# A 64x64 triangular inverse put together from two 64x64 factors in three visits instead of from 32x32 quarters in four

## The chip, the core and the metric

The kernel runs on one core of a Trainium2 chip. The metric is the device time of one execution in microseconds. The profile is one execution taken by the hardware profiler. Engines: PE is TensorE (matmuls), PEld its weight loads, DVE is VectorE, ACT is ScalarE, POOL is GpSimd. SP (SyncE) and ACT also issue DMAs, from their queues SPq and ACTq.

## What is computed

One block of a hybrid sequence model on 256 tokens of width 2048, in float32. The input is normalised and multiplied by a wide matrix; three branches follow (an RWKV-7 branch, a Mamba-2 branch, a short convolution), each is projected and gated, and the sum is projected again, added to the input and normalised. Only the RWKV-7 branch is touched by the change. Its recurrence is, for each of 16 heads of width 64:

```
def step(s, inp):
    r_t, w_t, k_t, v_t, kh_t, b_t = inp
    sa = jnp.einsum('bhvk,bhk->bhv', s, kh_t)
    s = s * w_t[:, :, None, :] - sa[..., None] * b_t[:, :, None, :] + v_t[..., None] * k_t[:, :, None, :]
    return s, jnp.einsum('bhvk,bhk->bhv', s, r_t)
```

The kernel does it in chunks of 64 tokens. Inside a chunk the term with `sa` couples each token to the earlier ones, so a strictly lower triangular 64x64 system has to be inverted for each head and chunk.

## The kernel before

**The main stream.** PE works through the big projections in "half chunks": eight matmuls on one tile of weights, four pairs of a 512-column product with the high parts (line 1353) and a 256-column product with the low parts (line 1356). A half chunk is one slot `t`; a main iteration `j` has 40 slots and handles one 128-channel tile, that is two heads (e) of the RWKV branch. There are seven such iterations in a loop and an eighth written out (`main(j, False)`, `main(CT - 1, True)`). Weights come in by DMA from SP into a ring of four buffers `raw`; ACT rounds them to `whi` (line 454, 128x1024) and DVE subtracts to get `wlo` (line 848, 128x1024), once in every two slots. All engines run their own program in the order in which it is written; semaphores tie them.

**The branch work hangs between the slots.** After some half chunks PE makes a short "visit": a handful of small float32 matmuls for the recurrence. A visit belongs to slot `t`, and the waits of the visit (`ready_behind(t)`) stand ahead of the last `wlo` matmul of that half chunk, so that a late partner holds the main stream itself. `V_P1` is 18.

**The inverse.** Each iteration has two heads (e), two blocks of 128 tokens (b) and two chunks in each (c). The four groups (b, e) are numbered q. For each chunk the 16x16 diagonal blocks are inverted on DVE in 32 partitions (`solve_step`, `solve_corner`; the last write is the copy of line 1155, semaphore `sol_tr`). The results and their transposes lie in `sol_2` and are spread over 128 partitions by DMA into `tb`: SP issues two DMAs (line 303) and ACT two (line 603), each 128 runs of 128 bytes. DVE multiplies `tb` by the block mask `par` to get `tx` (line 1078), block diagonal in 32 columns (two 16x16 blocks). From there:

- slot 18: `p1` = off-diagonal scores (`s4`) times the transposed small inverses, 32x32 (line 1584); before it the visit does `rk_mm` (1571) and `xv_mm` (1578); DVE adds the identity (1088)
- slot 19: the 32x32 inverses and their transposes (1593, 1596); ACT and DVE copy them out (673, 201)
- slot 20: `g_mm` (1605), slot 21: `h_mm` (1615), the lower left 32x32 quarter of the 64x64 inverse; ACT copies each (681, 684)
- slot 22: `uw_mm` (1623) uses the finished 64x64 inverse `t64`.

DVE in the same slots also does the causal convolution (864), the bonus products (1091, 1093), `shift` (881), `fold` (854), the gate of z (1168) and the segment products (1039).

Of the kernel before, what the change touches and what calls it, by code (L numbers as in the profile page):

```python
# [13 lines left out]
P = 128  # L14
D = 2048
T = 256
# [48 lines left out]
def build_program(nc, x, norm_w, w_in, rw_mu, rw_w0, rw_w2, rw_a0, rw_a2, rw_kk, rw_ka, rw_rk, rw_ln_w, rw_ln_b,  # L65
# [3 lines left out]
    with ctx:  # L69
# [52 lines left out]
        tx = lot(28).rearrange("p (q w n) -> p q w n", q=4, w=2)  # L122
        p1 = lot(29)[:, 0:P].rearrange("p (q n) -> p q n", q=4)
# [35 lines left out]
        par = sb("par", [P, 2, BLK])  # L159
        id32 = sb("id32", [P, 32])  # L160
# [10 lines left out]
        adt = sb("adt", [P, 4, CL])  # L171
        ad = sb("ad", [P, 4, BLK])
        t64 = sb("t64", [P, 4, 64])
        zeros = sb("zeros", [P, 256 + NC * (CL + 1)])
        t1, g1 = (zeros[:, n * P:(n + 1) * P].rearrange("p (q n) -> p q n", q=4) for n in range(2))
# [21 lines left out]
        def quad(n):  # L197
            return slice(32 * n, 32 * n + 32)

        def block_at(copy, i, *function):  # L200
            return copy(t64[quad(i), :, 32 * (i % 2):32 * (i % 2) + 32].rearrange("p (e b) n -> p e b n", e=2),
                        ps[quad(i), 4:6, 0:64].rearrange("p e (b n) -> p e b n", b=2), *function)

# [21 lines left out]
        names = """zeros_z f_sum z_ok pad_z const_z const_b const_m const_o prm_t prm_ok prm_d x_sq x_rt x_rs x_n x_tr h_hi h_lo ranks_sh lr_ok  # L225
# [3 lines left out]
            ad_ok n_in sol_p sol_r sol_tr t_in tx_ok p1_mm p1_ok d_mm t1_ok t64_ok  # L229
            xv_mm xv_ok g_mm g_ok h_mm h_ok uw_mm uw_ok yz_mm yz_ok z_in nm_mm  # L230
# [8 lines left out]
        def _(sp):  # L239
# [46 lines left out]
            def main(j, last):  # L286
# [15 lines left out]
                for q in range(2):  # L302
                    sp.dma_start(tb[:, q, :, :], sol_2[8 * q:8 * q + 8, :, :, :]).then_inc(s["t_in"], 16)
# [51 lines left out]
        def _(pool):  # L355
# [52 lines left out]

            pool.wait_ge(s["sc_mm"], NG)
            gp.memset(t64[:], 0.0).then_inc(s["pad_z"], 1)  # L410
# [15 lines left out]
        def _(act):  # L426
# [161 lines left out]
            def main(j, last):  # L588
# [8 lines left out]
                for t in range(2 * (LAST + GATES) if last else SLOTS):  # L597
                    if t % 2 == 0 and t // 2 < nchunks and t != 24:
                        split(t // 2 + AHEAD)
                    if t == 16:  # L600
                        act.wait_ge(s["sol_tr"], j + 1)
                        for q in range(2, 4):
                            act.dma_start(tb[:, q, :, :], sol_2[8 * q:8 * q + 8, :, :, :]).then_inc(s["t_in"], 16)
# [211 lines left out]
        def _(dve):  # L815
# [25 lines left out]
            v.tensor_reduce(id32[:], ident[:].rearrange("p (a n) -> p n a", a=4), AX.X, ALU.add)  # L841
            v.tensor_reduce(par[:].rearrange("p h u -> p (h u)"), m16b.rearrange("p (a n) -> p n a", a=4), AX.X, ALU.add
# [146 lines left out]
            def main(j, last):  # L989
# [45 lines left out]

                def seg_times(e, b):
# [6 lines left out]
                for t in range(2 * (LAST + GATES) if last else SLOTS):  # L1043
# [725 lines left out]
```

## Time and profile before

| | |
|---|---|
| median of 3 runs | 1118.74 us (1118.48 to 1118.74) |
| span of the profiled execution | 1119.5 us |
| PE busy / DVE / ACT | 99% / 72% / 55% of the span |
| chain that ended last | PE 98% of the span |
| granted TensorE clock, mean | 0.997 |

The profile gives for its execution the span from the first to the last instruction; no separate device time is shown for it, and the median of the runs lies 0.8 us below the span.

### The profile page before, as it was taken

To read this page: it belongs to the slowest core of one execution; us is meant where nothing else is said; L and a number is where in the kernel's file an instruction comes from. 1 tells how busy PE (TensorE), PEld (TensorE's weight loads), DVE (VectorE), ACT (ScalarE), POOL (GpSimd) and SP (SyncE) were. 2 spreads that over 40 slices of the span, in tenths; PEclk is the share of its full clock that TensorE was granted. 3 is DMA by queue.
4 is the path that set the end of the run, shared out by engine and by line. 5 is a ranking of instruction groups with operands and counts; after the bars stand their busy time and mean duration, and the time that the engine had idled before them with its cause. 6 is when DMAs were issued, how large, how long until landed. Compare 5 with 4: busy or idle time off the path is not lost.

```text
span 1119.5 us, 23001 instructions
## 1 busy us (share of the span) xinstructions
PE 1106.4 (99%) x8054; PEld 923.2 (82%) x8054; DVE 802.8 (72%) x1243; ACT 611.5 (55%) x931; POOL 44.4 (4%) x72
## 2 busy tenths in 40 slices
PE   8999999999999999999999999999999999999997
PEld 6888888888888888888888788888888888888885
DVE  4788889888897988879888857545555555556564
ACT  5656576565756657566565645444344444435443
POOL 3000000000000000000000030000000000000000
PEclk9999999999999999999999999999999999999999
DMA  7666656566465564756556464766666576657663
GB/s 199 188 170 170 176 136 174 158 169 165 131 172 161 157 176 124 192 146 173 145 156 182 141 203 151 225 191 196 196 189 192 164 225 192 199 182 279 200 194 107
DMA packets 254412, 197.25 MB, mean 176 GB/s; under 512 B 23095, under 2 KB 206624, under 8 KB 253856
## 3 DMA queue, kind: packets, MB, share of 16 engines
q1 hardware_dynamic: 251604, 195.81, 60.2%
q10 hardware_dynamic: 2764, 0.85, 0.3%
q8 instruction: 27, 0.44, 0.2%
q14 instruction: 17, 0.14, 0.0%
HBM read 193.71 MB, written 2.11 MB: 175 GB/s over the span
## 4 chain that ended last, share of the span: by engine, by line
PE 98%; DMA 0%; ACT 0%; SPq 0%; DVE 0%; issue 0%
PE ps L1353 31%; PE ps L1356 15%; PE ps L1452 12%; PE ps L1454 12%; PE ps L1453 12%; PE ps L1739 3%; PE ps L1738 3%; PE ps L1740 3%; PE ps L1486 1%; PE ps L1663 1%; PE ps L1336 1%; PE ps L1522 0%; PE ps L1383 0%; DMA o<-in_x 0%; PE ps L1623 0%; PE ps L1687 0%
## 5 line engine op out<-in xcount | busy, mean ns | idle before, releaser
L848 DVE TENSOR_TENSOR wlo<-raw,whi 128x1024 fp32r<-128x1024 f32 (+1 forms) x356 | 437.4, 1241 | 215.0 <-ACT whi L454 212.9
L1353 PE MATMUL ps<-hx,whi 128*128 128x512 f32 (+1 forms) x1440 | 522.9, 405 | 0.0
L454 ACT ACTIVATE whi<-raw 128x1024 fp32r<-128x1024 f32 (+1 forms) x356 | 370.3, 1051 | 252.7 <-PE ps L1454 178.7
L1356 PE MATMUL ps<-hx,wlo 128*128 128x256 f32 (+1 forms) x1440 | 404.1, 281 | 0.0
L1353 PEld LDWEIGHTS ps<-hx,whi 128*128 128x128 f32 (+1 forms) x1440 | 269.1, 187 | 70.2 <-issue 5.4
L1356 PEld LDWEIGHTS ps<-hx,wlo 128*128 128x128 f32 (+1 forms) x1440 | 270.8, 188 | 0.4
L1452 PE MATMUL ps<-whi,hx 128*128 128x512 f32 x384 | 150.3, 391 | 0.0
L1454 PE MATMUL ps<-whi,hx 128*128 128x512 f32 x384 | 149.5, 389 | 0.0
L1453 PE MATMUL ps<-wlo,hx 128*128 128x512 f32 x384 | 149.4, 389 | 0.0
L1452 PEld LDWEIGHTS ps<-whi,hx 128*128 128x128 f32 x384 | 72.1, 188 | 15.0 <-issue 0.2
L1454 PEld LDWEIGHTS ps<-whi,hx 128*128 128x128 f32 x384 | 72.1, 188 | 15.0
L1453 PEld LDWEIGHTS ps<-wlo,hx 128*128 128x128 f32 x384 | 72.1, 188 | 14.8
L1454 PE MATMUL ps<-whi,olo 128*128 128x512 f32 x192 | 74.7, 389 | 0.0
L1452 PE MATMUL ps<-whi,ohi 128*128 128x512 f32 x192 | 74.7, 389 | 0.0
L1453 PE MATMUL ps<-wlo,ohi 128*128 128x512 f32 x192 | 74.7, 389 | 0.0
L1738 PE MATMUL ps<-whi,hx 128*128 128x512 f32 x128 | 50.0, 390 | 0.0
L1740 PE MATMUL ps<-whi,hx 128*128 128x512 f32 x128 | 49.8, 389 | 0.0
L1739 PE MATMUL ps<-wlo,hx 128*128 128x512 f32 x128 | 49.8, 389 | 0.0
L1453 PEld LDWEIGHTS ps<-wlo,ohi 128*128 128x128 f32 x192 | 36.0, 188 | 7.5
L1452 PEld LDWEIGHTS ps<-whi,ohi 128*128 128x128 f32 x192 | 36.0, 188 | 7.5
L1454 PEld LDWEIGHTS ps<-whi,olo 128*128 128x128 f32 x192 | 36.0, 188 | 7.4
L467 ACT ACTIVATE lots<-ps 128x256 f32<-128x256 f32 x48 | 17.5, 382 | 39.5 <-issue 20.1
(281 smaller groups left out, 1040.3 us busy)
## 6 DMA issues: line engine op xcount, KB each, us to landing
raw<-in_w_in SPq DMA_DIRECT2D x548, 256.0 KB, 3.2
raw<-in_w_branch SPq DMA_DIRECT2D x96, 256.0 KB, 3.8
raw<-in_w_out SPq DMA_DIRECT2D x64, 256.0 KB, 3.6
o<-in_x SPq DMA_DIRECT2D x3, 1024.0 KB, 6.1
acb<-acs_rows SPq DMA_DIRECT2D x7, 256.0 KB, 3.3
out_y<-lots SPq DMA_DIRECT2D x5, 256.0 KB, 2.6
o<-in_x SPq DMA_DIRECT2D x2, 512.0 KB, 5.3
lots<-in_final_norm_w SPq DMA_DIRECT2D x1, 1024.0 KB, 10.2
```

What stands on the lines that cost most here:

```text
L454: sc.activation(whi[:, slot, :, 0:width], raw[:, slot, :, 0:width], ACT.Copy).then_inc(hi_done, 1)
L467: sc.activation(dst, ps[:, bank + t, T:2 * T], ACT.Copy).then_inc(low_out, 1)
L848: tt(wlo[:, slot, :, 0:width], raw[:, slot, :, 0:width], whi[:, slot, :, 0:width].bitcast(F32), ALU.subtract).then_inc(lo_done, 1)
L1336: return mm(ps[:, X_BANK[k % 6], b * P:(b + 1) * P], xtok[:, b, k * P:(k + 1) * P], rdiag[:, b, :], start=True, stop=True)
L1353: mm(ps[0:rows, bank, :], whi[:, slot, k, wcol], hx[:, kt].rearrange("p a t -> p (a t)"), start=first, stop=False, skip_group_check=True)
L1356: return mm(ps[0:rows, bank, 0:T], wlo[:, slot, k, wcol], hhi[:, kt, :], start=False, stop=last, skip_group_check=True)
L1452: mm(dst, xh[:, kt, r], whi_o[:, slot, k, :], start=kt == 0, stop=False)
L1453: mm(dst, xh[:, kt, r], wlo_o[:, slot, k, :], start=False, stop=False)
L1454: op = mm(dst, xl[:, kt, r], whi_o[:, slot, k, :], start=False, stop=kt == 2 * nq - 1)
L1738: mm(dst, hhi[:, kt, r], whi_o[:, y % RING, k, :], start=kt == 0, stop=False)
L1739: mm(dst, hhi[:, kt, r], wlo_o[:, y % RING, k, :], start=False, stop=False)
L1740: op = mm(dst, hlo[:, kt, r], whi_o[:, y % RING, k, :], start=False, stop=kt == KT - 1)
```

## The change

The 64x64 inverse is written as a product of two factors. With T the block diagonal of the 16x16 inverses and N the strictly-off-block part of the scores, M = T N has 4x4 blocks and its fourth power vanishes, so that the inverse is (1 + M^2)(1 + M) T. Every product is now 64x64 by 64, on the four 64x64 quarters of the array.

- `tx` becomes block diagonal in 64 columns: its own buffer, written 128x512 instead of 128x256. `par` has four columns of blocks instead of two.
- Slot 18: line 1584's 16 products of 32x32 go; in their place 16 products of 64x64 (`m_mm`: M and its transpose for all eight chunk-heads).
- Slot 19: the visit goes (24 products of 32x32), and so do its four copies; ACT copies M and its transpose out (`mx`, 128x512), DVE adds the identity (`mi`, 128x256). DVE no longer makes `p1`.
- Slot 20: 16 products of 64x64 (`k_mm`: M^2 and (1 + M) T) in place of 8 of 32x32.
- Slot 21: 8 products of 64x64 (`t_mm`) in place of 8 of 32x32. Before it ACT copies `kg` (128x256) and DVE makes 1 + M^2 (`m2i`, 128x256); after it ACT copies `t64` (128x256) in one piece.
- The rows of `tb` for odd heads have to lie on the other half of the partitions for one of the two kinds, so that one of the two DMAs of SP, and one of ACT, is split in three: SP and ACT issue four DMAs each instead of two.
- The zeroing of `t64` by POOL at the start goes.

```
                 sp.wait_ge(s["sol_tr"], j + 1)
-                for q in range(2):
-                    sp.dma_start(tb[:, q, :, :], sol_2[8 * q:8 * q + 8, :, :, :]).then_inc(s["t_in"], 16)
+                sp.dma_start(tb[:, 0, :, :], sol_2[0:8, :, :, :]).then_inc(s["t_in"], 16)
+                sp.dma_start(tb[:, 1, 1, :], sol_2[8:16, :, 1, :]).then_inc(s["t_in"], 16)
+                for h in range(CPB):
+                    sp.dma_start(tb[side(1 - h), 1, 0, :], sol_2[8 + 4 * h:12 + 4 * h, :, 0, :]).then_inc(s["t_in"], 16)
...
                     if t == V_P1 + 1:
+                        act.wait_ge(s["m_mm"], j + 1)
+                        sc.activation(mx.rearrange("p e w b n -> p e (w b n)"), ps[:, 4:6, 0:T], ACT.Copy).then_inc(s["mx_ok"], 1)
                         act.wait_ge(s["xv_mm"], j + 1)
                         act.wait_ge(s["bon_ok"], j + 1)
                         sc.activation(xx4[:, :, 1:3, :].rearrange("p b e n -> p e b n"),
                                       ps[:, 6:8, 0:P].rearrange("p e (b n) -> p e b n", b=2), ACT.Copy).then_inc(s["xv_ok"], 1)
-                        act.wait_ge(s["d_mm"], j + 1)
-                        for i in (0, 2):
-                            op = sc.activation(t1[quad(i), :, :], A[quad(i), 64:64 + P].rearrange("p (q n) -> p q n", q=4), ACT.Copy)
-                        op.then_inc(s["t1_ok"], 1)
-                        act.wait_ge(s["pad_z"], 1)
-                        for i in (0, 2):
-                            op = block_at(sc.activation, i, ACT.Copy)
-                        op.then_inc(s["t64_ok"], 1)
                     if t == V_P1 + 3:
-                        act.wait_ge(s["g_mm"], j + 1)
-                        sc.activation(g1.rearrange("p (e b) n -> p e (b n)", e=2), ps[:, 6:8, 0:64], ACT.Copy).then_inc(s["g_ok"], 1)
-                        act.wait_ge(s["h_mm"], j + 1)
-                        for i in (0, 2):
-                            op = sc.activation(t64[quad(i), :, 32:64], A[quad(i), 0:P].rearrange("p (q n) -> p q n", q=4), ACT.Copy)
-                        op.then_inc(s["h_ok"], 1)
+                        act.wait_ge(s["k_mm"], j + 1)
+                        sc.activation(kg, blocks(6, 0), ACT.Copy).then_inc(s["kg_ok"], 1)
+                        act.wait_ge(s["t_mm"], j + 1)
+                        sc.activation(t64[:], blocks(4, 0), ACT.Copy).then_inc(s["t64_ok"], 1)
...
-                        dve.wait_ge(s["t_in"], j * 64 + 64)
-                        tt(tx.rearrange("p q w (h u) -> p (q w) h u", h=2),
-                           tb[:].rearrange("p q w u -> p (q w) u").unsqueeze(2).broadcast_to([P, 8, 2, BLK]),
-                           par[:].unsqueeze(1).broadcast_to([P, 8, 2, BLK]), ALU.mult).then_inc(s["tx_ok"], 1)
+                        dve.wait_ge(s["t_in"], j * 128 + 128)
+                        tt(tx[:].rearrange("p q w (h u) -> p (q w) h u", h=4),
+                           tb[:].rearrange("p q w u -> p (q w) u").unsqueeze(2).broadcast_to([P, 8, 4, BLK]),
+                           par[:].unsqueeze(1).broadcast_to([P, 8, 4, BLK]), ALU.mult).then_inc(s["tx_ok"], 1)
...
                     if t == V_P1 + 1:
 
-                        dve.wait_ge(s["p1_mm"], j + 1)
-                        tt(p1, B[:, 0:P].rearrange("p (q n) -> p q n", q=4), id32[:].unsqueeze(1).broadcast_to([P, 4, 32]),
-                           ALU.add).then_inc(s["p1_ok"], 1)
+                        dve.wait_ge(s["m_mm"], j + 1)
                         dve.wait_ge(s["rk_mm"], j + 1)
                         tt(bon[:, 0:P], C[:, T:T + P], sh[:, 2, 0:P], ALU.mult)
                         for e in range(2):
                             op = tt(bon[side(e), P:T], E[side(1 - e), T + P:2 * T], sh[side(e), 2, P:T], ALU.mult)
                         op.then_inc(s["bon_ok"], 1)
                     if t == V_P1 + 1:
-                        dve.wait_ge(s["d_mm"], j + 1)
-                        dve.wait_ge(s["pad_z"], 1)
-                        for i in (1, 3):
-                            op = block_at(v.tensor_copy, i)
-                        op.then_inc(s["t64_ok"], 1)
+
+                        dve.wait_ge(s["mx_ok"], j + 1)
+                        plus_one(mi, mx[:, :, 1, :, :]).then_inc(s["mi_ok"], 1)
+                    if t == V_P1 + 3:
+
+                        dve.wait_ge(s["k_mm"], j + 1)
+                        plus_one(m2i, blocks(4, T)).then_inc(s["m2i_ok"], 1)
...
-                    if t == V_P1 + 1:
-                        pe.wait_ge(s["p1_ok"], j + 1)
                     if t == V_P1 + 2:
-                        pe.wait_ge(s["t1_ok"], j + 1)
+                        pe.wait_ge(s["mx_ok"], j + 1)
+                        pe.wait_ge(s["mi_ok"], j + 1)
                         pe.wait_ge(s["xv_ok"], j + 1)
                     if t == V_P1 + 3:
-                        pe.wait_ge(s["g_ok"], j + 1)
-                        pe.wait_ge(s["t64_ok"], j * 2 + 2)
+                        pe.wait_ge(s["kg_ok"], j + 1)
+                        pe.wait_ge(s["m2i_ok"], j + 1)
                     if t == V_P1 + 4:
-                        pe.wait_ge(s["h_ok"], j + 1)
+                        pe.wait_ge(s["t64_ok"], j + 1)
...
-                        for q in range(4):
-                            for i in range(4):
-                                r = slice(32 * i, 32 * i + 32)
-                                op = mm(B[r, 32 * q:32 * q + 32], s4[r, q, 2 * CL + 32 * (i % 2):2 * CL + 32 * (i % 2) + 32], tx[r, q, 1, :],
-                                        start=True, stop=True)
-                        op.then_inc(s["p1_mm"], 1)
-                    if t == V_P1 + 1:
-
-                        for q in range(4):
-                            b, e = q // 2, q % 2
-                            for i in range(4):
-                                r, o = quad(i), quad(i ^ 2 * e)
-                                mm(ps[o, 4 + e, 32 * b:32 * b + 32], p1[r, q, :], tx[r, q, 0, :], start=True, stop=True)
-                            for i in (0, 2):
-                                r, x = quad(i), 64 + 32 * (2 * e + b)
-                                op = mm(A[r, x:x + 32], tx[r, q, 0, :], p1[r, q, :], start=True, stop=True)
-                        op.then_inc(s["d_mm"], 1)
-                    if t == V_P1 + 2:
-
-
                         for b in range(2):
                             for c in range(CPB):
                                 for e in range(2):
-                                    r, o = quad(2 * c), quad(2 * (c ^ e) + 1)
-                                    op = mm(ps[o, 6 + e, 32 * b:32 * b + 32],
-                                            s4[r, 2 * b + e, 2 * CL + 32:3 * CL], t1[r, 2 * e + b, :],
+                                    r, q, n = side(c), 2 * b + e, b * CL
+                                    off = s4[r, q, 2 * CL:3 * CL]
+                                    mm(ps[side(c ^ e), 4 + e, n:n + CL], tx[r, q, 1, :], off, start=True, stop=True)
+                                    op = mm(ps[side(c ^ e), 4 + e, P + n:P + n + CL], off, tx[r, q, 1, :], start=True, stop=True)
+                        op.then_inc(s["m_mm"], 1)
+                    if t == V_P1 + 2:
+
+
+                        for b in range(2):
+                            for c in range(CPB):
+                                for e in range(2):
+                                    r, n = side(c ^ e), b * CL
+                                    mm(ps[side(c), 4 + e, T + n:T + n + CL], mx[r, e, 0, b, :], mx[r, e, 1, b, :],
+                                       start=True, stop=True)
+                                    op = mm(ps[side(c), 6 + e, n:n + CL], mi[r, e, b, :], tx[r, 2 * b + e, 0, :],
                                             start=True, stop=True)
-                        op.then_inc(s["g_mm"], 1)
+                        op.then_inc(s["k_mm"], 1)
                     if t == V_P1 + 3:
 
 
-                        for q in range(4):
-                            for h in range(2):
-                                r = quad(2 * h + 1)
-                                op = mm(A[quad(2 * h), 32 * q:32 * q + 32], g1[r, q, :], t64[r, q, 32:64], start=True, stop=True)
-                        op.then_inc(s["h_mm"], 1)
+                        for b in range(2):
+                            for c in range(CPB):
+                                for e in range(2):
+                                    op = mm(ps[side(c ^ e), 4 + e, b * CL:b * CL + CL], m2i[side(c), e, b, :], kg[side(c), e, b, :],
+                                            start=True, stop=True)
+                        op.then_inc(s["t_mm"], 1)
```

The four hunks after the first are ACT, DVE (two) and the waits ahead of the last `wlo` matmul on PE; the last is the visits of PE. How the instructions then stand on the engines is shown at three places; the line numbers of the changed kernel are its own.

DVE, from the split of slot 18 to the split of slot 20. Before:

```order
L848 TENSOR_TENSOR wlo<-raw,whi 128x1024 [waits hi_done]
L1088 TENSOR_TENSOR lots<-ps,id 128x128 [waits p1_mm]
L1091 TENSOR_TENSOR lots<-ps,lots 128x128 [waits rk_mm]
L1093 TENSOR_TENSOR lots<-ps,lots 64x128 x2
L201 COPY t<-ps 32x4x32 [waits pad_z,d_mm]
L201 COPY t<-ps 32x4x32
L847 REGISTER_ALU
L848 TENSOR_TENSOR wlo<-raw,whi 128x1024 [waits hi_done]
```

and in the changed kernel (line 1027 with `adt` is `mi`):

```order
L837 TENSOR_TENSOR wlo<-raw,whi 128x1024 [waits hi_done]
L1082 TENSOR_TENSOR lots<-ps,lots 128x128 [waits rk_mm,m_mm]
L1084 TENSOR_TENSOR lots<-ps,lots 64x128 x2
L1027 TENSOR_TENSOR adt<-lots,id 128x256 [waits mx_ok]
L836 REGISTER_ALU
L837 TENSOR_TENSOR wlo<-raw,whi 128x1024 [waits hi_done]
```

The addition of `p1` and the two copies behind `d_mm` are gone; one addition behind `mx_ok` stands ahead of the split.

DVE, from `shift` of slot 20 to the segment products of slot 21. Before:

```order
L881 SCALAR_TENSOR_TENSOR lots<-pq,prm,lots 128x256
L853 REGISTER_ALU
L854 TENSOR_TENSOR lots<-ps,lots 128x256 [waits low_out]
L853 REGISTER_ALU
L854 TENSOR_TENSOR lots<-ps,lots 128x256 [waits low_out]
L1167 REGISTER_ALU
L1168 SCALAR_TENSOR_TENSOR lots<-lots 128x256 [waits halved]
L1039 ISA [waits seg_e,dat_ok]
```

and in the changed kernel (line 1027 with `zeros` is `m2i`):

```order
L870 SCALAR_TENSOR_TENSOR lots<-pq,prm,lots 128x256
L842 REGISTER_ALU
L843 TENSOR_TENSOR lots<-ps,lots 128x256 [waits low_out]
L842 REGISTER_ALU
L843 TENSOR_TENSOR lots<-ps,lots 128x256 [waits low_out]
L1160 REGISTER_ALU
L1161 SCALAR_TENSOR_TENSOR lots<-lots 128x256 [waits halved]
L1027 TENSOR_TENSOR zeros<-ps,id 128x256 [waits k_mm]
L1032 ISA [waits seg_e,dat_ok]
```

`m2i`, for which PE waits in slot 21, stands behind the split, the shift, two folds and the gate of slot 20.

ACT, from its DMAs of slot 16 on (in the last iteration). Before:

```order
L603 DMA tb<-lots 128x1x32 [waits sol_tr]
L603 DMA tb<-lots 128x1x32
L467 ACTIVATE lots<-ps 128x256 [waits tile_done]
L467 ACTIVATE lots<-ps 128x256 [waits chunk_used]
L470 ACTIVATE lots<-xp,prm 128x256 [waits tile_out]
L645 ACTIVATE lots<-lots 128x256 [waits tile_out]
L454 ACTIVATE whi<-raw 128x1024 [waits chunk_used,raw_in3]
L669 ACTIVATE lots<-ps 128x2x2x64 [waits bon_ok,xv_mm]
L673 ACTIVATE zeros<-ps 32x128 [waits d_mm]
```

and in the changed kernel:

```order
L596 DMA tb<-lots 128x1x32 [waits sol_tr]
L597 DMA tb<-lots 128x1x16
L599 DMA tb<-lots 64x1x16 x2
L461 ACTIVATE lots<-ps 128x256 [waits tile_done]
L461 ACTIVATE lots<-ps 128x256 [waits chunk_used]
L464 ACTIVATE lots<-xp,prm 128x256 [waits tile_out]
L642 ACTIVATE lots<-lots 128x256 [waits tile_out]
L448 ACTIVATE whi<-raw 128x1024 [waits chunk_used,raw_in3]
L665 ACTIVATE lots<-ps 128x512 [waits m_mm]
L668 ACTIVATE lots<-ps 128x2x2x64 [waits bon_ok,xv_mm]
L448 ACTIVATE whi<-raw 128x1024 [waits chunk_used,raw_in0]
```

Four DMA issues stand where two stood; the copy of M (line 665) is new, and the split of slot 20 now follows directly on the copy of `xv` (line 668). SP's queue changes in the same way as ACT's, and the rest of the weights' DMAs stand behind.

## Rows read from the trace of the kernel before

**Rows 1.** The page: the span, and the chain that ended last by engine.

```profile
span 1119.5 us, 23001 instructions
...
PE 98%; DMA 0%; ACT 0%; SPq 0%; DVE 0%; issue 0%
```

**Rows 2.** Waits of PE, whole run: who for whom, us in total, times, longest.

```profile
PE ps L1336 <- DVE lots L826: 3.4, 2, 1.9
PE ps L1331 <- DVE zeros L819: 1.5, 1, 1.5
```

**Rows 3.** Timeline of PE, second iteration, slots 18 to 22: start, us, instruction, count.

```profile
200.18 0.28 PE L1356 MATMUL ps<-hx,wlo 128*128 128x256 f32 x1
200.29 0.40 PE L1353 MATMUL ps<-hx,whi 128*128 128x512 f32 x1
200.52 0.28 PE L1356 MATMUL ps<-hx,wlo 128*128 128x256 f32 x1
...
201.00 0.41 PE L1578 MATMUL ps<-lots,work 64*64 64x64 f32 x16
201.34 0.45 PE L1584 MATMUL ps<-lots,work 32*32 32x32 f32 x32
201.72 0.50 PE L1353 MATMUL ps<-hx,whi 128*128 128x512 f32 x1
...
203.12 0.28 PE L1356 MATMUL ps<-hx,wlo 128*128 128x256 f32 x1
...
203.88 0.50 PE L1353 MATMUL ps<-hx,whi 128*128 128x512 f32 x1
...
205.27 0.28 PE L1356 MATMUL ps<-hx,wlo 128*128 128x256 f32 x1
...
205.74 0.51 PE L1353 MATMUL ps<-hx,whi 128*128 128x512 f32 x1
...
207.14 0.28 PE L1356 MATMUL ps<-hx,wlo 128*128 128x256 f32 x1
...
207.72 0.51 PE L1353 MATMUL ps<-hx,whi 128*128 128x512 f32 x1
```

**Rows 4.** Timeline of DVE, the same stretch (idle time before in brackets).

```profile
199.17 0.43 DVE L1078 TENSOR_TENSOR lots<-tb,par 128x256 f32<-128x256 f32 x1 [0.91 <-DMA tb<-lots]
199.51 0.48 DVE L864 SCALAR_TENSOR_TENSOR lots<-xp,prm,lots 128x256 f32<-128x256 f32 x1
...
201.18 1.22 DVE L848 TENSOR_TENSOR wlo<-raw,whi 128x1024 fp32r<-128x1024 f32 x1
202.31 0.28 DVE L1088 TENSOR_TENSOR lots<-ps,id 128x128 f32<-128x128 f32 x1
202.52 0.28 DVE L1091 TENSOR_TENSOR lots<-ps,lots 128x128 f32<-128x128 f32 x1
202.81 0.59 DVE L1093 TENSOR_TENSOR lots<-ps,lots 64x128 f32<-64x128 f32 x2
...
206.23 1.23 DVE L848 TENSOR_TENSOR wlo<-raw,whi 128x1024 fp32r<-128x1024 f32 x1 [1.64 <-ACT whi L454]
...
208.88 1.40 DVE L1039 SCALAR_TENSOR_TENSOR lots<-lots,dat,scm 128x256 f32<-128x256 f32 x4
```

**Rows 5.** Timeline of ACT, the same stretch.

```profile
203.50 0.38 ACT L669 ACTIVATE lots<-ps 128x256 f32<-128x256 f32 x1 [3.76 <-DVE lots L1093]
...
205.13 1.06 ACT L454 ACTIVATE whi<-raw 128x1024 fp32r<-128x1024 f32 x1
```

**Rows 6.** Timeline of the two DMA queues: start, us for all issues, line, count.

```profile
196.02 1.27 ACTq L603 DMA_DIRECT2D tb<-lots  x2
...
196.02 1.53 SPq L303 DMA_DIRECT2D tb<-lots  x2
...
181.52 2.77 SPq L295 DMA_DIRECT2D lots<-ad  x4
```

**Rows 7.** Line 267, DMAs of 64 partitions: issue time in ns, min/median/max.

```profile
L267 SPq DMA_DIRECT2D lorat<-in_rw_w x8: 479/547/556, 13.3 to 545.7; - x8
```

More of the change, by code:

```diff
@@ L121, in build_program @@
         yz = flat(26, 2).rearrange("p (q n) -> p q n", q=4)
-        tx = lot(28).rearrange("p (q w n) -> p q w n", q=4, w=2)
-        p1 = lot(29)[:, 0:P].rearrange("p (q n) -> p q n", q=4)
+        mx = flat(28, 2).rearrange("p (e w b n) -> p e w b n", e=2, w=2, b=2)
+        kg = lot(32).rearrange("p (e b n) -> p e b n", e=2, b=2)
         yc, ysq = lot(29), lot(12)
@@ L158, in build_program @@
         m16b = lot(13)[:, 0:P]
-        par = sb("par", [P, 2, BLK])
-        id32 = sb("id32", [P, 32])
+        par = sb("par", [P, 4, BLK])
+        id64 = sb("id64", [P, CL])
+        tx = sb("tx", [P, 4, 2, CL])
         head1 = sb("head1", [P, P])
@@ L171, in build_program @@
         adt = sb("adt", [P, 4, CL])
+        mi = adt[:, :, :].rearrange("p (e b) n -> p e b n", e=2)
         ad = sb("ad", [P, 4, BLK])
-        t64 = sb("t64", [P, 4, 64])
+        t64 = sb("t64", [P, 2, 2, CL])
         zeros = sb("zeros", [P, 256 + NC * (CL + 1)])
-        t1, g1 = (zeros[:, n * P:(n + 1) * P].rearrange("p (q n) -> p q n", q=4) for n in range(2))
+        m2i = zeros[:, 0:256].rearrange("p (e b n) -> p e b n", e=2, b=2)
         steps = zeros[:, 256:].rearrange("p (c t) -> p c t", c=NC)
@@ L195, in side, with blocks @@
             return slice(64 * n, 64 * n + 64)
[L197 to L202, printed above, removed]
+        def blocks(bank, col):
+            return ps[:, bank:bank + 2, col:col + P].rearrange("p e (b n) -> p e b n", b=2)
         BANKS = (0, 2, 0, 0, 2)
@@ L224, in build_program @@
         low_out = sem("low_out")
-        names = """zeros_z f_sum z_ok pad_z const_z const_b const_m const_o prm_t prm_ok prm_d x_sq x_rt x_rs x_n x_tr h_hi h_lo ranks_sh lr_ok
+        names = """zeros_z f_sum z_ok const_z const_b const_m const_o prm_t prm_ok prm_d x_sq x_rt x_rs x_n x_tr h_hi h_lo ranks_sh lr_ok
             bc_s bc_th bc_ok sc_mm scm_ok dt_v dt_e dt_l dt_ae acs_ok
@@ L228, in build_program @@
             kh_ok ka_t k2_ok rk_ok rk_mm bon_ok bon_b bv_ok prod_ok tr_vk vt_ok kdbd_ok score_mm score_ok adt_ok
-            ad_ok n_in sol_p sol_r sol_tr t_in tx_ok p1_mm p1_ok d_mm t1_ok t64_ok
-            xv_mm xv_ok g_mm g_ok h_mm h_ok uw_mm uw_ok yz_mm yz_ok z_in nm_mm
+            ad_ok n_in sol_p sol_r sol_tr t_in tx_ok m_mm mx_ok mi_ok k_mm kg_ok m2i_ok t_mm t64_ok
+            xv_mm xv_ok uw_mm uw_ok yz_mm yz_ok z_in nm_mm
             nm_ok state_mm state_ok y_mm yc_ok ysq_ok var_mm var_rt ln_v oa_ok sc_cx sc_s sc_b sc_f oc_hi oc_ok x_s xs_ok z2_ok x_tr2 xst_ok
@@ L407, in main @@
                     kk_unit(j + 1)
-            pool.wait_ge(s["sc_mm"], NG)
-            gp.memset(t64[:], 0.0).then_inc(s["pad_z"], 1)
             kk_unit(0)
@@ L601, in main @@
                         act.wait_ge(s["sol_tr"], j + 1)
-                        for q in range(2, 4):
-                            act.dma_start(tb[:, q, :, :], sol_2[8 * q:8 * q + 8, :, :, :]).then_inc(s["t_in"], 16)
+                        act.dma_start(tb[:, 2, :, :], sol_2[16:24, :, :, :]).then_inc(s["t_in"], 16)
+                        act.dma_start(tb[:, 3, 1, :], sol_2[24:32, :, 1, :]).then_inc(s["t_in"], 16)
+                        for h in range(CPB):
+                            act.dma_start(tb[side(1 - h), 3, 0, :], sol_2[24 + 4 * h:28 + 4 * h, :, 0, :]
+                                          ).then_inc(s["t_in"], 16)
                     if t >= 2 * nchunks:
@@ L840, in _ @@
             stt(centre[:], head1[:], -1.0 / 64, ident[:], ALU.mult, ALU.add)
-            v.tensor_reduce(id32[:], ident[:].rearrange("p (a n) -> p n a", a=4), AX.X, ALU.add)
-            v.tensor_reduce(par[:].rearrange("p h u -> p (h u)"), m16b.rearrange("p (a n) -> p n a", a=4), AX.X, ALU.add
+            v.tensor_reduce(id64[:], ident[:].rearrange("p (a n) -> p n a", a=2), AX.X, ALU.add)
+            v.tensor_reduce(par[:].rearrange("p h u -> p (h u)"), m16b.rearrange("p (a n) -> p n a", a=2), AX.X, ALU.add
                             ).then_inc(s["const_o"], 1)
@@ L1034, in solve_corner, with plus_one @@
                     v.tensor_reduce(dst, prod, AX.X, ALU.add).then_inc(s["sol_r"], 1)
+                def plus_one(dst, src):
+                    return tt(dst, src, id64[:].unsqueeze(1).unsqueeze(1).broadcast_to([P, 2, 2, CL]), ALU.add)
                 def seg_times(e, b):
@@ L1622, in main @@
                                 for e in range(2):
-                                    op = mm(ps[side(h ^ e), 4 + e, b * P:b * P + P], t64[side(h), 2 * e + b, :],
+                                    op = mm(ps[side(h ^ e), 4 + e, b * P:b * P + P], t64[side(h), e, b, :],
                                             xx[side(h), (2 * b + e) * P:(2 * b + e) * P + P], start=True, stop=True)
```

## The prediction, written before the changed kernel ran

> **What bounds the kernel now.** I read the page first: the chain that ended last is PE for 98% of 1119.5 us [rows 1]. Then the waits of PE: in the whole run it waited twice, for 4.9 us in all, both times in the first microseconds (its first operands, zeroed and scaled by DVE) [rows 2]. In the main iterations PE never waits. So two questions decide the change: does PE's own work get shorter, and does any partner that PE has so far never waited for come too late? What nobody waits for today may be late by little, so next I read the timelines of PE, DVE and ACT for slots 18 to 22 of the second iteration, one beside the other. The other seven have the same shape; their gaps differ by under 0.2 us.
>
> **PE's own work.** A visit's cost is the gap between the last `wlo` matmul ahead of it and the first `whi` matmul behind it, less the 0.11 us that stand between the two without a visit (200.18 to 200.29) [rows 3].
> - Slot 19 goes whole: 203.12 to 203.88 is 0.76, less 0.11: -0.65.
> - Slot 18: the old 32 instructions (each float32 product is two) took 0.38 (201.34 to 201.72). Thirty-two of 64x64 stand there now. The nearest row is line 1578, the same shape on the same four quarters: 16 in 0.34 (201.00 to 201.34), 21 ns each, which includes the change to narrow products behind it. By that price it is 0.68 (+0.30); the lower bound is the 32-wide price, 12 ns (+0). That change of width goes, so I take +0.1.
> - Slot 20: 32 in place of 16. 205.27 to 205.74 is 0.47, less 0.11 is 0.36 with its start. Bounds: 16 more at 12 ns (+0.2) and 32 at 21 ns against 16 at 16 (+0.42). I take +0.3.
> - Slot 21: 16 in place of 16; before they used two tiles of the array and now use four, twice as wide. Bounds -0.2 and 0; I take -0.05.
>
> Sum: -0.3 us an iteration (bounds -0.7 and +0.05, all ends at once), over eight iterations -2.4 us. If nothing else moved, that would be all.
>
> **What the new steps wait for.** Now the partners, in order of time.
>
> *The DMAs.* `tx` waits for the `tb` DMAs: DVE stood idle 0.91 us for them, then started `tx` at 199.17 [rows 4]. Issuing is slow: two took ACT 1.27 us and two took SP 1.53 us, both from 196.02 on; four of 128 runs of 64 bytes took SP 2.77 us, 0.69 each; one of 64 partitions takes 0.547 us [rows 6, 7]. The new set on each queue is one like before, one of 128 short runs and two of 64 short runs. On SP: 0.77 + 0.69 + 2 x 0.55 = 2.56 against 1.53, so the last issue ends 1.03 us later. Bounds for what isn't shown, a short issue of 64 runs: half of 0.69 (the sum is 2.15, +0.6), and the 0.77 of an issue when both queues issue at once, for all four (3.06, +1.5). I take a delay d of 1.15 us, because both queues issue together for longer.
>
> At this place a rule of the Trainium skill speaks for a smaller price. The page "DMA: Bandwidth & Descriptors", section "Issuing engines are not separate DMA queues", says that the time an engine's sequencer needs to start a DMA is usually small relative to the DMA itself. By it the two more issues would cost nearly nothing, and the sum would be that of the second rival below; the trace does not agree for these tiny transfers, where an issue takes 0.64 to 0.77 us.
>
> *tx.* It starts at 199.17 + d and is 128x512. From 128x256 (0.43) and 128x1024 (1.22) [rows 4] it should take 0.43 + 0.26 = 0.69. PE needs it ahead of its last `wlo` matmul of slot 18, at 200.52 [rows 3]. It is there at 199.17 + 1.15 + 0.69 + 0.05 = 201.06: PE **waits 0.5 us** where it never waited.
>
> *bon, mi, xv.* DVE goes on with three convolution steps and the split of slot 18, without a gap after `tx`, so they shift by d + 0.26. Then `p1` is gone (202.31 to 202.52: -0.21) [rows 4]. The bonus products, which ended at 202.81 + 0.59 = 203.40, end at 203.45 + d = 204.60. `mi` follows, 0.43, at 205.03; the copy of `xv` on ACT (0.10 behind, 0.38 long [rows 5]) ends at 205.08. PE asks for both ahead of the last matmul of slot 20: 205.27 + 0.5 + 0.1 - 0.65 = 205.22. Just in time; a late one here would be swallowed by the next wait anyway. The copy of M on ACT (twice the width of a 0.38 us copy, begun about 202.5) is done before the bonus products are.
>
> *m2i.* This one is the crux. The order shows it behind five instructions on DVE, the first of which is the split of slot 20, which waits for ACT's `whi`; ACT does that `whi` behind the copy of `xv`. It used to stand behind the four copies of slot 19, and now comes earlier. ACT: copy ends 203.93 + d; DVE's split starts 1.10 after ACT's (205.13 to 206.23) [rows 4, 5]: 205.03 + d. From the start of that split to the first instruction behind the gate of z DVE takes 206.23 to 208.88, 2.65 us, with no wait inside [rows 4]: `m2i` starts at 207.68 + d, takes 0.43 like any 128x256, and PE has it at 208.16 + d. PE's last matmul of slot 21 stood at 207.14 [rows 3]. So PE passes this point **1.02 + d later than before**, whatever happened in slots 18 to 20: the gain of slot 19 and the wait of slot 18 are both inside. With d = 1.15 it is 2.17 late, at 209.31; it would arrive at 205.22 + 0.3 + (207.14 - 205.27) = 207.39, so **it waits 1.9 us**. Queued behind that waiting matmul is the whole main stream.
>
> *After it.* The visit of slot 21 saves 0.05. `t64` is one copy of 0.38 us, with a half chunk of 1.4 us ahead of its use. ACT and DVE lose less than PE, so their slack grows: nothing else turns late. SP issues the remaining weights of that strip about 1 us later; they are split on ACT in slots 22 and after, some 7 us behind their landing. The edits outside the loop (two reductions 64 wide instead of 32, one zeroing less on POOL) are hundredths of a microsecond.
>
> **The sum.** Per iteration 1.02 + 1.15 - 0.05 = 2.12 us; over eight 17.0. The profiled execution's span goes from 1119.5 to 1136.5; the median of the runs lies 0.8 below the span, 1118.7 + 17.0 = 1135.7.
>
> **The rivals.**
> 1. *As summed, both waits.* With d from 0.6 to 1.5, an iteration costs 1.6 to 2.5 us: 1131.3 to 1138.7. Chance 0.73.
> 2. *The DMAs are not later* (short issues cheap, or overlapped with the moving of data): d near 0 to 0.4. Then `tx` is in time and only `m2i` is late: 0.97 us an iteration, 7.8 in all: 1126.5, up to 1130. For it: the moved bytes grow by nothing. Against it: every issue row. Chance 0.11.
> 3. *Faster.* `m2i` is in time. PE without waits gets to that matmul at 207.14 - 0.65 + 0.1 + 0.3 = 206.89, so DVE would have to be 1.3 us faster than the 208.16 it needs even with d = 0; from there on only PE's sum counts, -2.4 us: 1116.3 (1113 to 1119 by the bounds). For it: it is what PE's own rows say, PE is 98% of the chain, and both ACT and DVE have idle gaps of 1.6 us and more here. Against it: the order of DVE's program, and those gaps are the ones I have already closed. Chance 0.06.
> 4. *Near no change*, the same with a wait of some tenths. Chance 0.03.
> 5. *More than summed*: small DMAs that land later still behind twice as many issues on both queues, or a wait in slot 20 or 24 as well; at 2.8 us an iteration 1141. Chance 0.07.
>
> The first case's own range is 1131 to 1139; with the upper part of the second and the nearest of the fifth it is 1127 to 1140, which leaves out about 2 in 10. About 0.2% (2.2 us) is what a measurement can tell here from no change. Slower by more: 0.73 + 0.11 + 0.07 = 0.91. Faster 0.06, same 0.03.
>
> **What the profile after would show.** Waits of PE on DVE that did not exist: one of about 0.5 us, eight times, released by the `tx` product (waited for in slot 18), and one of about 1.9, eight times, released by the addition of 1 to M^2 (slot 21). The last of the `tb` issues of SP ending about 1 us later, `tx` at about 0.69 us for 128x512. The gap of slot 19's visit closed to 0.11. If the `m2i` wait is missing, my reading of DVE's queue is wrong; if it is 1.0 to 1.5 and the first wait is missing, the DMAs were priced too high. If a wait in slot 20 shows and slot 21's is shorter by as much, the sum stands. Matmul groups 64 wide well over 21 ns an instruction would make only the waits shorter, not the time longer.

## The result

The changed kernel takes 1136.72 us (median of 5 runs, 1136.44 to 1137.94), the kernel before 1118.74 (5 runs beside it, 1118.48 to 1119.77). Ratio 1.0161, 95% interval 1.015 to 1.0173: 18 us slower, where 17 were forecast.

The page of the changed kernel, span and chain by engine, against [rows 1]:

```profile
span 1134.9 us, 22487 instructions
...
PE 81%; DVE 9%; issue 4%; DMA 2%; SPq 2%; ACT 1%; DVEq 1%; ACTq 0%
```

PE was 98% of the chain that ended last and is 81%; DVE, the DMAs and ACT have come into it. The waits of PE (who for whom, us in total, times, longest), against [rows 2]:

```profile
PE ps L1349 <- DVE zeros L1027: 10.4, 8, 1.4
PE ps L1349 <- DVE tx L1071: 5.4, 8, 0.8
PE ps L1329 <- DVE lots L815: 2.8, 2, 1.4
```

Two waits that did not exist, each eight times: for `m2i` (the addition of line 1027 into `zeros`) and for `tx`. The timeline of PE in the second iteration, against [rows 3]:

```profile
200.01 0.40 PE L1346 MATMUL ps<-hx,whi 128*128 128x512 f32 x1
201.10 0.35 PE L1349 MATMUL ps<-hx,wlo 128*128 128x256 f32 x1 [0.69 <-DVE tx L1071]
...
202.56 0.50 PE L1346 MATMUL ps<-hx,whi 128*128 128x512 f32 x1
...
205.37 0.28 PE L1349 MATMUL ps<-hx,wlo 128*128 128x256 f32 x1
205.58 0.36 PE L1588 MATMUL ps<-lots 64*64 64x64 f32 x8
...
206.26 0.50 PE L1346 MATMUL ps<-hx,whi 128*128 128x512 f32 x1
...
207.42 0.40 PE L1346 MATMUL ps<-hx,whi 128*128 128x512 f32 x1
209.12 0.35 PE L1349 MATMUL ps<-hx,wlo 128*128 128x256 f32 x1 [1.31 <-DVE zeros L1027]
209.41 0.46 PE L1599 MATMUL ps<-lots,zeros 64*64 64x64 f32 x16
209.80 0.50 PE L1346 MATMUL ps<-hx,whi 128*128 128x512 f32 x1
```

Without a wait the low product follows 0.24 us behind the high one (207.66); it came at 209.12, 1.46 us late. DVE in the same stretch, against [rows 4]:

```profile
195.33 0.38 DVE L1148 COPY lots<-lots 32x256 f32<-32x256 f32 x1
...
200.26 0.69 DVE L1071 TENSOR_TENSOR tx<-tb,par 128x512 f32<-128x512 f32 x1 [2.28 <-DMA tb<-lots]
...
204.59 0.43 DVE L1027 TENSOR_TENSOR adt<-lots,id 128x256 f32<-128x256 f32 x1
206.02 1.23 DVE L837 TENSOR_TENSOR wlo<-raw,whi 128x1024 fp32r<-128x1024 f32 x1 [1.00 <-ACT whi L448]
...
208.22 0.42 DVE L1161 SCALAR_TENSOR_TENSOR lots<-lots 128x256 f32<-128x256 f32 x1
208.56 0.42 DVE L1027 TENSOR_TENSOR zeros<-ps,id 128x256 f32<-128x256 f32 x1
```

This is the queue the forecast spoke of: M^2 is on PE's side finished before 206.26, and its addition starts at 208.56, behind the split, the shift, the folds and the gate. DVE has no idle time ahead of it after 206.02. And SP's DMA queue, against [rows 6]:

```profile
195.74 0.69 SPq L297 DMA_DIRECT2D tb<-lots  x1
196.47 0.79 SPq L298 DMA_DIRECT2D tb<-lots  x1
197.31 1.49 SPq L300 DMA_DIRECT2D tb<-lots  x2
```

The four issues end at 198.80, 3.47 us behind the copy of 195.33, instead of two at 197.55, 1.95 behind the copy of 195.60 (line 1155 in the trace of before).

**The period is the better ruler.** The last write of the small inverses (the copy of line 1155 in before, `sol_tr`) occurs once in an iteration; first and last start, seven periods apart. Of before and of the changed kernel:

```profile
L1155 DVE COPY lots<-lots x8: 384/385/387, 127.1 to 606.1; 32x256 f32<-32x256 f32 x8
```

```profile
L1148 DVE COPY lots<-lots x8: 384/386/391, 124.5 to 619.9; 32x256 f32<-32x256 f32 x8
```

68.43 us before (479.0 / 7) and 70.77 after (495.4 / 7): 2.34 us an iteration, 18.7 over eight. The changed kernel's first copy lies 2.6 us earlier than in the profile of before, which is why the span grew by only 15.4. An experiment below shows that this is the one execution of before, not the change.

### The profile page after: what moved, and what is told of

Read it like the earlier page. It is cut to its first block, busy times and chain, and to the rows that moved or that the text cites. A ratio compares the mean times of both kernels' runs of the same rounds, so it can differ in the third digit from the quotient of the medians.

```text
span 1134.9 us, 22487 instructions
## 1 busy us (share of the span) xinstructions
PE 1106.7 (98%) x7798; PEld 924.2 (81%) x7798; DVE 805.5 (71%) x1235; ACT 605.2 (53%) x899; POOL 44.1 (4%) x71
## 4 chain that ended last, share of the span: by engine, by line
PE 81%; DVE 9%; issue 4%; DMA 2%; SPq 2%; ACT 1%; DVEq 1%; ACTq 0%
PE ps L1346 21%; PE ps L1445 12%; PE ps L1446 12%; PE ps L1447 12%; PE ps L1349 11%; PE ps L1725 3%; PE ps L1723 3%; PE ps L1724 3%; DVE lots L1019 2%; DMA tb<-lots 2%; DVE wlo L837 1%; DVE lots L1008 1%; DVE lots L1010 1%; ACT whi L448 1%; DVE lots L853 1%
```

## The experiments

Periods here are worked out as above from the same copy's line in each trace.

### The addition of M^2 ahead of DVE's other work

```
+                    if t == V_P1 + 2:
+                        dve.wait_ge(s["k_mm"], j + 1)
+                        plus_one(m2i, blocks(4, T)).then_inc(s["m2i_ok"], 1)
                     if t % 2 == 0 and t // 2 < nchunks and t not in (V_ST, V_ST + 2):
                         split_lo(base + t // 2 + AHEAD, (t // 2 + AHEAD) % RING)
...
-                    if t == V_P1 + 3:
-
-                        dve.wait_ge(s["k_mm"], j + 1)
-                        plus_one(m2i, blocks(4, T)).then_inc(s["m2i_ok"], 1)
```

> The changed kernel with one addition moved: DVE makes 1 + M^2 (m2i) ahead of the weight split of slot 20 instead of behind split, shift, two folds and gate. Theory A (the wait of slot 21 is set by DVE's order): M^2 is there at about 206.4 in the second iteration, m2i at 206.9, and PE reaches its last matmul of slot 21 at 207.66 instead of 209.12. The wait on m2i goes, 1.46 us an iteration and some tenths of restart over all eight: 1124.5 to 1125.5 us. The wait for tx of 0.7 us stays. Theory B (the cost is the wider products on PE, or weights that arrive later since SP issues more): no change from 1136.7.

Measured 1124.38 us, just under the expected range, ratio to before 1.0048 (1.0033 to 1.0064), period 69.19. Of the two waits of PE in the iterations one is left:

```profile
PE ps L1348 <- DVE tx L1074: 5.4, 8, 0.8
```

One instruction's place in DVE's program was worth 12.3 us. The products, the copies and the DMAs are the same in both kernels, so theory B falls.

### Two DMAs on each queue again

```
-                sp.dma_start(tb[:, 1, 1, :], sol_2[8:16, :, 1, :]).then_inc(s["t_in"], 16)
-                for h in range(CPB):
-                    sp.dma_start(tb[side(1 - h), 1, 0, :], sol_2[8 + 4 * h:12 + 4 * h, :, 0, :]).then_inc(s["t_in"], 16)
+                sp.dma_start(tb[:, 1, :, :], sol_2[8:16, :, :, :]).then_inc(s["t_in"], 16)
```

and the same on ACT.

> The changed kernel with two tb DMAs on each queue, as before the change; the odd heads' untransposed 16x16 inverses then lie on the wrong half of the partitions, so that part of the RWKV branch is computed from other blocks. Theory A (issue time of the DMAs delays tx, and through DVE's order m2i): tx starts 1.37 us earlier, its wait on PE is gone, and m2i comes 1.37 earlier, still 1.0 us late for PE: 1125 to 1126.5 us. A rival that only the wait for tx itself counts (0.69 us an iteration) gives 1131; if the DMAs do not matter, 1136.7.

Measured 1126.25 us, ratio 1.0064 (1.0049 to 1.008), period 69.39. The wait for `tx` is gone, the one for `m2i` stays, shorter:

```profile
PE ps L1344 <- DVE zeros L1022: 6.5, 8, 0.9
```

The gain is 1.38 us an iteration, not the 0.69 of the wait that vanished: the DMAs delayed all of DVE's queue, `m2i` with it. That tells the forecast's account from the one that counts only the visible wait of slot 18 (1131). It is also the case of the forecast's second rival, DMAs that are not later: that rival had 7.8 us above the kernel before, and here are 7.5. The second iteration:

```profile
194.00 0.39 DVE L1143 COPY lots<-lots 32x256 f32<-32x256 f32 x1
...
206.43 0.36 PE L1344 MATMUL ps<-hx,wlo 128*128 128x256 f32 x1 [0.84 <-DVE zeros L1022]
```

The low product of slot 21 stands 12.43 us behind the copy of the small inverses, against 11.54 before (207.14 less 195.60).

### Both edits

> The last two edits together (the odd heads' blocks are again on the wrong half of the partitions). No wait of PE should be left, and what remains is PE's own work. The prediction's products (-0.3 us an iteration) give 1116.3; the products as the trace of the changed kernel shows them (slot 18 +0.18, slot 20 +0.42, slot 21 +0.02, slot 19 -0.65) give nearly nothing, 1117.5 to 1118.7. If a further wait was hidden behind the two, it shows here and the time stays above 1119.

Measured 1117.62 us, ratio 0.999 (0.9981 to 0.9999), period 68.24. No wait of PE in the iterations is left. Together the two edits take away 2.53 us an iteration, alone 1.58 and 1.38: less than their sum, since in `m2i_early` the DMAs' delay counts only through `tx`. What remains is PE's own work: 0.1 to 0.2 us an iteration less than before the change. The time fits the products as the trace has them, and not the forecast's -0.3 (1116.3).

### The old kernel with four DMAs on each queue

The edit of the change on its own: the second DMA split in three on SP and on ACT, with each half in its old place, and the count waited for doubled.

> The kernel before the change, the same data moved by four tb DMAs on each queue instead of two (one of 128 runs of 64 bytes and two of 64 such runs in place of the second). It shows the price of the issues alone. Theory A: tx starts 1.4 us later, at 200.5; PE waits 0.5 us in slot 18, then 0.3 to 0.4 in slot 19 for p1, which DVE makes behind it: 0.9 us an iteration, 1126 us (1124 to 1128). The rule that issuing is small beside the transfer gives no change, 1118.7.

Measured 1127.07 us, ratio 1.0071 (1.0056 to 1.0086), period 69.51, that is 1.1 us an iteration, the bytes unchanged. The split also cuts the second DMA's runs from 128 bytes to 64 and doubles their number, so the price could lie in the transfer as well. The timeline says where it lies (second iteration, SP's last two issues and `tx`):

```profile
196.46 1.51 SPq L305 DMA_DIRECT2D tb<-lots  x2
```

```profile
199.44 0.43 DVE L1083 TENSOR_TENSOR lots<-tb,par 128x256 f32<-128x256 f32 x1 [2.30 <-DMA tb<-lots]
```

From the end of the last issue to `tx` it is 1.47 us here, 1.62 in before (197.55 to 199.17): the transfers behind the last issue did not get longer, the issues alone made `tx` late. In its timeline of PE:

```profile
200.01 0.35 PE L1361 MATMUL ps<-hx,wlo 128*128 128x256 f32 x1 [0.41 <-DVE lots L1083]
...
202.45 0.39 PE L1358 MATMUL ps<-hx,whi 128*128 128x512 f32 x1
202.92 0.39 PE L1361 MATMUL ps<-hx,wlo 128*128 128x256 f32 x1
```

The wait for `tx` in slot 18, and 0.23 us more in slot 19 (0.47 from high to low product instead of 0.24) for `p1`, which DVE makes 3 us behind `tx`. The second is too short to leave idle time in the records, and shows in the starts alone. The rest, up to the 1.1, is in the two visits, which are longer behind a matmul that waited (1.28 us against 1.20 from the low product to the next high one in slot 18, 0.87 against 0.76 in slot 19).

### tx in two pieces: a complete kernel without the delay

```
-                        dve.wait_ge(s["t_in"], j * 128 + 128)
...
+                        dve.wait_ge(s["t_in"], j * 64 + 64)
+                        spread(1).then_inc(s["tx_ok"], 1)
...
+                    if t == V_P1:
+                        dve.wait_ge(s["t0_in"], j * 64 + 64)
+                        spread(0).then_inc(s["tx0_ok"], 1)
```

`spread(w)` is the product of `tx` for one w; the half DMAs count on `t0_in`; `m2i` is made early.

> A complete kernel with neither wait: m2i early, and tx made in two pieces. The first two DMAs of each queue already bring all transposed blocks (w = 1), all that slot 18 needs; DVE spreads these at once (128x256). The four half DMAs have a semaphore of their own, and DVE spreads the w = 0 blocks after the split of slot 18; PE asks for them in slot 20. Theory A: t_in is complete as early as before the change, nothing waits, the period of an iteration is that of both_waits_off (68.2 us): 1117.6 us (1117 to 1118.3), 1 us below the kernel before. If the moved half of tx (0.34 us more on DVE ahead of mi) or the later weights' DMAs of SP cost something, it is 1118.5 to 1121.

Measured 1118.56 us, ratio 0.9995 (0.9986 to 1.0004), period 68.46: no change from before that can be told, a little short of what was expected. Both big waits are gone. What is left is in DVE's timeline, second iteration:

```profile
197.91 0.48 DVE L853 SCALAR_TENSOR_TENSOR lots<-xp,prm,lots 128x256 f32<-128x256 f32 x1 [0.53 <-ACT lots L464]
...
200.72 0.42 DVE L1027 TENSOR_TENSOR tx<-tb,par 128x256 f32<-128x256 f32 x1
201.06 0.28 DVE L1092 TENSOR_TENSOR lots<-ps,lots 128x128 f32<-128x128 f32 x1
```

The first convolution step stands 0.5 us idle for the first tap, which ACT makes behind its four DMA issues, and the moved half of `tx` takes 0.34 us ahead of the bonus products (200.72 to 201.06). The second is the rival that the expectation named. The bonus products, and behind them the copy of `xv` and `mi`, are later by both, and PE's last low product of slot 20 comes 0.26 instead of 0.24 behind the high one here, more in other iterations and 0.73 in the first; the visit behind it takes 0.97 instead of 0.90.

### The order of the products

The same kernel with the loops of slots 18 and 20 turned, so that four products in a row use four quarters of the array.

> The last kernel with the products of slots 18 and 20 issued so that neighbours never use the same quarter of the array (M for all four quarters, then its transpose; M^2 for four, then the other product). In the changed kernel two products in a row use one quarter; their instructions start 67 ns apart for a round of four, where line 1578 of before has 58. If the neighbours cost that difference, 16 rounds save 0.15 us an iteration: 1116.4. If each quarter has its own queue and the order is nothing, 1117.6 as the last.

Measured 1117.88 us, ratio 0.9993 (0.9984 to 1.0002), period 68.37. The medians differ by 0.7 us, less than the intervals are wide. In the traces the 32 instructions of slot 18 stand so:

```profile
198.89 0.30 PE L1586 MATMUL ps<-work,tx 64*64 64x64 f32 x8
...
199.47 0.50 PE L1352 MATMUL ps<-hx,whi 128*128 128x512 f32 x1
```

0.58 us, against 0.67 in the changed kernel (201.89 to 202.56): the turned order saves 0.09 us there. That neighbours in one quarter cost something is what this says. What slot 18 gained PE lost again at its next wait, for `xv` and `mi` in slot 20:

```profile
202.04 0.39 PE L1352 MATMUL ps<-hx,whi 128*128 128x512 f32 x1
202.45 0.36 PE L1355 MATMUL ps<-hx,wlo 128*128 128x256 f32 x1
```

The low product comes 0.41 us behind the high one, and in both kernels it stands 9.2 us behind the copy of the small inverses. What the order is worth where nothing waits is seen in `late_halves`.

### The kernel before once more

> The kernel before, unchanged, profiled once more. The profile of before reached its first solved blocks (line 1155) at 127.1 us, all later kernels at 124.5 to 125.7, though their code ahead of it is nearly the same. If that is chance of one execution, it is near 124.6 here, and the span is about 1117; if the constants of the changed kernel make the start faster, it stays at 127.1 and the span at 1119.5.

Measured 1118.65 us. The profile:

```profile
span 1116.5 us, 23001 instructions
```

with the first copy at 124.6 and a period of 68.37 (603.2 less 124.6, by 7). So the first profile of before had a start slower by 2.5 us by chance; the median of the runs does not have it. Its main iterations agree within 0.06 us a period, and its low products of slots 18 to 21 stand at the same places behind the copy within 0.05 us. It also sets the forecast's step from span to time right: the time of a run is some 1.7 us above its span (1118.24 and 1116.5 here, 1136.66 and 1134.9 for the changed kernel), and not 0.8 below it, as the first profile beside the median had suggested. The forecast started from the median, so its time is untouched; its span, 1136.5, was not met by the measured 1134.9.

### The halves issued later

```
-                        for h in range(CPB):
-                            act.dma_start(tb[side(1 - h), 3, 0, :], sol_2[24 + 4 * h:28 + 4 * h, :, 0, :]
-                                          ).then_inc(s["t0_in"], 16)
...
                         first_tap(j, xp, cv)
+                        for h in range(CPB):
+                            act.dma_start(tb[side(1 - h), 3, 0, :], sol_2[24 + 4 * h:28 + 4 * h, :, 0, :]
+                                          ).then_inc(s["t0_in"], 16)
...
                         plus_one(mi, mx[:, :, 1, :, :]).then_inc(s["mi_ok"], 1)
+                        dve.wait_ge(s["t0_in"], j * 64 + 64)
+                        spread(0).then_inc(s["tx0_ok"], 1)
```

> tx_in_two_order with what its trace showed late put right: ACT issues its two half DMAs behind the first tap of the convolution instead of ahead of it (DVE stood idle 0.55 us for that tap, and PE then waited 0.1 to 0.2 us in slot 20 for the copy of xv), and DVE spreads the w = 0 blocks behind mi instead of ahead of the bonus products. Theory A: no wait of PE is left in the main iterations, the period falls from 68.3 to 68.1 or 68.2 us: 1117.0 us (1116.3 to 1117.6), 1.5 us below the kernel before. If the halves now land too late for slot 20, PE waits there for tx0 and the time is 1118 or more.

Measured 1115.88 us (9 runs, 1115.37 to 1117.16), ratio 0.9971 (0.9961 to 0.9981), period 68.11: faster than both kernels, more so than expected. In its timeline of PE, second iteration, the visit of slot 20 and its neighbours:

```profile
201.65 0.28 PE L1354 MATMUL ps<-hx,wlo 128*128 128x256 f32 x1
201.86 0.34 PE L1595 MATMUL ps<-lots 64*64 64x64 f32 x8
...
202.49 0.50 PE L1351 MATMUL ps<-hx,whi 128*128 128x512 f32 x1
```

and on ACT the copy of `xv`, and on DVE `m2i` waiting for PE, not the other way round:

```profile
200.24 0.39 ACT L668 ACTIVATE lots<-ps 128x256 f32<-128x256 f32 x1 [0.61 <-DVE lots L1091]
```

```profile
202.62 0.43 DVE L1033 TENSOR_TENSOR zeros<-ps,id 128x256 f32<-128x256 f32 x1 [1.69 <-PE ps L1600]
```

The bonus products start 6.63 us behind the copy of the small inverses, and 7.57 in `tx_in_two`: the 0.53 of the tap and the 0.34 of the half are both gone. From low product to next high one the visit of slot 20 takes 0.84 us, against 0.90 in `both_waits_off`, and that of slot 18 takes 1.29 against 1.39: with no wait left, the turned order shows in the period, 68.11 against 68.24. The two kernels differ in the DMAs and in `tx` too, and this one has two edits at once, so how much of the 3.1 us below before belongs to the order, to the later halves and to the later piece of `tx` was not measured one by one. Issuing the half DMAs from POOL's queue instead was not tried.

## Why the prediction was right

**PE passes slot 21 late by 1.02 + d.** Measured from the copy of the small inverses, the low product of slot 21 stood 11.54 us behind it before (207.14 less 195.60, where line 1155 starts in the first trace) and 13.79 after (209.12 less 195.33): 2.25 late; forecast 2.17. With the visit behind it 2.34 an iteration, forecast 2.12. `m2i_early` shows the wait is the order's, and its removal gives 1.58. The mechanism was right; that the number is as near as 0.08 is in part luck. d was 0.21 larger than forecast, and the 1.02 was 0.89: `dma_two`, where `tx` starts 3.57 us behind the copy as before and d is nothing, shows the same 0.89 (12.43 less 11.54). The 0.13 between are three small terms: DVE's split of slot 20 started 0.10 earlier than worked out (10.69 us behind the copy), DVE took 2.54 us from it to `m2i` (206.02 to 208.56) and not 2.65, and PE started 0.56 behind the start of `m2i` (209.12) and not 0.48.

**d, the delay of the DMAs: a term too small.** `tx` started 3.57 us behind that copy before and 4.93 after: 1.36, not 1.15. The step that was off is the price of an issue of 64 runs, taken as 0.55 from line 267: here the median is 0.72 on SP and 0.69 on ACT. SP's four issues took 3.06 us (195.74 to 198.80) where 2.56 were summed; 3.06 was the forecast's upper bound. Behind the copy, the last issue ended 1.52 later than before; from its end to `tx` it was 1.46 instead of 1.62, and so d stayed at 1.36. `dma_two` (1.38 an iteration) and `before_four` (1.1, with PE's later wait in slot 19 and not in slot 21) confirm what d does. In `before_four` the bytes were the same and the time grew by 8.3 us. The rule of the Trainium skill, "DMA: Bandwidth & Descriptors", section "Issuing engines are not separate DMA queues", that issuing is usually small beside the transfer, does not hold for these DMAs: an issue takes some 0.7 us here, and from the end of the last one to `tx` it is 1.47 us.

**tx.** 0.69 us for 128x512, as worked out. Its wait was forecast as 0.5. By the starts PE's low product came 0.85 us late (1.09 behind the high one instead of 0.24, of which the records show 0.69 as idle). Of the 0.3 too much, 0.2 is d; the rest is that PE started 0.15 us behind the end of `tx` (200.95 to 201.10), where 0.05 was taken.

**mi and xv in slot 20: just in time.** Right: no wait there, with `mi` done at 205.02 and the low product at 205.37.

**The wait for m2i: 1.9 forecast, 1.46 measured** (1.3 idle in the records). The sum does not suffer, since PE only came later to the same wait: by the longer wait of slot 18 and by products that cost more.

**PE's own work: -0.3 forecast, -0.1 to -0.2 measured.** This term was mis-sized, and the waits hid it. In the changed kernel slot 20's gap is 0.89 (205.37 to 206.26) against 0.47: +0.42, the upper bound that the row of line 1578 gave, where I took +0.3. Slot 18 with its wait out of the way is 0.19 dearer (1.39 in `both_waits_off`, 1.20 before), where I took 0.1; slot 21's 0.39 from first product to the next high one (209.41 to 209.80) is near what it was (0.37, 207.35 to 207.72 before). Slot 19 gives 0.75 and not 0.65, since the first low product behind a visit follows its high one by 0.34 us and not 0.24, which the forecast's way of reading a gap leaves out:

```profile
204.22 0.28 PE L1356 MATMUL ps<-hx,wlo 128*128 128x256 f32 x1
```

In before it is 1.10 us from one low product to the next across the visit (203.12 to 204.22), and 0.35 without one. The four terms add up to -0.12. `both_waits_off` measures the sum: 68.24 against 68.43 and 68.37, 0.1 to 0.2 us an iteration. The third rival's 1116.3 was therefore too good by about 1.3 us for the products in this order. In `late_halves`, with the order turned, slot 18 is 0.09 dearer than before and slot 20 0.37, and with slots 19 and 21 as above the sum is -0.27, near the forecast: those two terms of the forecast fit an order of products that the changed kernel did not have, which is luck.

**A cost left out.** The low product that has waited is longer to start its visit: 0.29 us from it to the first small product (201.10 to 201.39 for slot 18, 209.12 to 209.41 for slot 21), against 0.21 without a wait (205.37 to 205.58). Twice 0.08 an iteration, 1.3 us in all. With it the visit of slot 21 cost 0.10 more than before, where 0.05 less was forecast.

**A count misread.** In the whole run of before PE waited three times for the 4.9 us, not twice (the 2 in the first line of [rows 2] is a number of waits). All three lie in the first 15 us, so nothing rests on it.

**After it.** Nothing else turned late: no third wait of PE shows, and no wait of PE for weights shows. In `tx_in_two` DVE's wait for the first tap, behind ACT's issues, did appear; in the changed kernel it lies under the wait for the DMAs. The chip's answer for the whole design is `late_halves`: the three visits of 64x64 products, in their turned order, are worth 0.3% once no wait is left.

## What to carry to other kernels

Where one engine is the chain and waits for nobody, a new dependency is priced by the consumer's time, the producer's place in its own program and everything queued ahead of it there, not by its own 0.43 us; put such a small product first, ahead of long work that has slack. Count DMA issues on the path, not bytes: a transfer split in three pays for three. And when two late partners feed one another, the visible wait of the first is less than what it costs, so take them off one at a time and together.

## What the runs showed of the hardware

An issue of a small DMA between SBUF and SBUF takes about as long for 64 runs of 64 bytes (medians in the changed kernel 0.72 us on SP, 0.69 on ACT) as for 128 runs of 64 or 128 bytes (0.62 to 0.80). Where ACT issued its halves later in `late_halves`, they took less:

```profile
L661 ACTq DMA_DIRECT2D tb<-lots x16: 562/562/571, 127.0 to 603.8; - x16
```

The neighbour queue was not idle then. In the second iteration SP issued its own halves over the same time, ACT's starting at 194.76 and 195.35:

```profile
194.62 1.60 SPq L300 DMA_DIRECT2D tb<-lots  x2
```

So two queues issuing at once is not enough to make an issue dear; what does make the difference stays open.

In the changed kernel the products of lines 1578 and 1579 alternate in PE's program, each as two instructions. Their starts do not:

```profile
201.89 0.33 PE L1578 MATMUL ps<-work,tx 64*64 64x64 f32 x6
202.00 0.22 PE L1579 MATMUL ps<-tx,work 64*64 64x64 f32 x1
```

Six instructions of line 1578 stand ahead of the first of line 1579. In the turned order of `late_halves` the starts alternate in eights, as written.
